# GpSimd, not VectorE, adds row and mask of the mLSTM decays; a split wait and two reordered steps in a hybrid streaming layer

## The reference

```python
dm = where(tril, bh[:, None] - bh[None, :] + ig[None, :], -inf)    # decays
m_t = maximum(bh + m, max(dm, -1))                                 # running maximum
sc = (q @ k.T) * exp(dm - m_t[:, None])
num = sc @ v + exp(bh + m - m_t)[:, None] * (q @ C.T)
h = num / maximum(abs(den), exp(-m_t))[:, None]
```

## Time and profile before

| | |
|---|---|
| median of 3 runs | 944.44 us (944.26 to 945.87) |
| the profiled execution | 944.33 us, its span 942.5 us |
| mean granted clock of TensorE in it | 0.996 |
| TensorE busy | 926.9 us, 98% |
| VectorE / ScalarE / GpSimd busy | 52% / 22% / 47% |
| DMA | 113.02 MB, mean 120 GB/s |

### The profile page before, as it was taken

How to read it: one execution, slowest core, us unless ns; L and a number is a source line. 1 busy time by engine, 2 the same in 40 slices (tenths; PEclk the granted TensorE clock), 3 DMA queues, 4 the chain that set the end, 5 groups by cost and what they waited for, 6 DMA issues and landing times.

```text
span 942.5 us, 14894 instructions
## 1 busy us (share of the span) xinstructions
PE 926.9 (98%) x5718; PEld 813.5 (86%) x5718; DVE 493.8 (52%) x1009; ACT 203.9 (22%) x445; POOL 444.6 (47%) x469
## 2 busy tenths in 40 slices
PE   8999999999999999999999989999999999999998
PEld 6776777777999999999977667777789999999998
DVE  5473645854565656512253555478356565653221
ACT  2223245432100000100031243453320000001001
POOL 6210281033976666676411205603168666666770
PEclk9999999999999999999999999999999999999999
DMA  9958311319544444343443772212474444544321
GB/s 282 253 101 82 123 47 47 91 11 240 146 138 136 135 134 134 125 156 124 121 130 109 55 144 58 77 52 51 79 190 135 135 135 138 144 134 139 130 91 45
DMA packets 159635, 113.02 MB, mean 120 GB/s; under 512 B 10246, under 2 KB 157356, under 8 KB 159436
## 3 DMA queue, kind: packets, MB, share of 16 engines
q1 hardware_dynamic: 154660, 104.50, 38.3%
q0 software_dynamic: 4272, 6.80, 6.9%
q10 hardware_dynamic: 632, 0.75, 0.3%
HBM read 108.46 MB, written 2.27 MB: 117 GB/s over the span
## 4 chain that ended last, share of the span: by engine, by line
PE 89%; DMA 6%; DVE 3%; ACT 1%; issue 1%; POOL 0%; SPq 0%; DVEq 0%; ACTq 0%
PE ps L1126 51%; PE ps L774 14%; PE ps L1083 7%; DMA arena<-r 5%; PE ps L1144 2%; PE ps L883 1%; PE ps L980 1%; PE ps L920 1%; PE ps L822 1%; DMA arena<-in_x_sample 1%; PE ps L1021 1%; PE ps L802 1%; PE ps L1030 1%; PE ps L963 1%; PE ps L1064 0%
## 5 line engine op out<-in xcount | busy, mean ns | idle before, releaser
L774 PE MATMUL ps<-hT,ring 128*128 128x320 f32 x672 | 190.4, 440 | 2.2 <-DVE hT L1595 1.7
L774 PEld LDWEIGHTS ps<-hT,ring 128*128 128x128 f32 x672 | 126.1, 192 | 55.9 <-issue 4.5
L601 POOL TENSOR_TENSOR work<-ring 128x512 f32<-128x512 f32 (+1 forms) x66 | 81.8, 1239 | 153.6 <-issue 113.3
L1126 PE MATMUL ps<-mixT,ring 128*128 128x160 f32 x672 | 105.0, 299 | 0.0
L1126 PE MATMUL ps<-hT,work 128*128 128x160 f32 x672 | 98.5, 299 | 0.0
L1126 PE MATMUL ps<-hT,ring 128*128 128x160 f32 x672 | 98.1, 299 | 0.0
L1126 PEld LDWEIGHTS ps<-mixT,ring 128*128 128x128 f32 x672 | 95.8, 190 | 0.0
L1126 PEld LDWEIGHTS ps<-hT,ring 128*128 128x128 f32 x672 | 93.7, 190 | 0.3
L1126 PEld LDWEIGHTS ps<-hT,work 128*128 128x128 f32 x672 | 93.7, 190 | 0.0
L603 POOL TENSOR_TENSOR work<-ring 128x512 f32<-128x512 f32 (+1 forms) x66 | 82.3, 1248 | 5.2
L602 POOL TENSOR_TENSOR ring<-ring 128x512 f32<-128x512 f32 (+1 forms) x66 | 82.2, 1246 | 5.2
(11 more groups left out here) (392 smaller groups left out, 1351.3 us busy)
## 6 DMA issues: line engine op xcount, KB each, us to landing
ring<-in_w_gu SPq DMA_DIRECT2D x88, 512.0 KB, 5.2
ring<-in_w_in SPq DMA_DIRECT2D x44, 512.0 KB, 6.2
ring<-in_w_down SPq DMA_DIRECT2D x32, 512.0 KB, 4.4
ring<-in_w_out SPq DMA_DIRECT2D x16, 512.0 KB, 4.4
ring<-in_w_down SPq DMA_DIRECT2D x16, 384.0 KB, 3.7
cst<-in_consts POOLq DMA_DIRECT2D x1, 1664.0 KB, 11.6
ring<-in_w_in SPq DMA_DIRECT2D x2, 640.0 KB, 5.6
arena<-r POOLq DMA_DIRECT2D x8, 160.0 KB, 17.1
```

Of the source, the lines that this page charges most:

```text
L601: step(tt(s3, a11, a21, ALU.subtract))
L774: ins = mm(bank(use, 0, T, m), w[:, k, c:c + m], hT[:, k, 0:T], start=(k == 0), stop=(k == KT - 1))
L1126: ins = mm(bank(use, at * HT, HT), left, right(k), start=(opens and k == 0 and at == 0), stop=(closes and k == n - 1), skip_group_check=True)
```

## The change

It has five parts.

1. The broadcasts of heads 0 and 1 count on the semaphore `tables_loaded`, those of heads 2 and 3 on `latents_loaded`. `decay_arg(0)` and `decay_arg(1)` wait for the first two alone, the others for all.
2. `decay_arg` goes from VectorE to GpSimd. There heads 0 and 1 stand behind the signal `b_out`; heads 2 and 3 stand in the loop over states, each ahead of the wait for the state two heads back. Each head but the first waits for the last one's exponentials, since `dmx` is one buffer. ScalarE waits for `w_d` of head h - 2 before it overwrites `dh[h % 2]`.
3. TensorE turns the mLSTM output ahead of `weigh_values(0)` and no longer at the start of head 1.
4. VectorE gates it (`group_out`) ahead of `b_out(0)`, not behind it.
5. ScalarE copies the turned probabilities of head 1 ahead of the second value copy of C.

```diff
@@ setup @@
-        NSMALL = len(SMALL)
+        NTABLES = 16 * (len(SMALL[5::2]) + 1)
@@ GpSimd @@
                 need(pool, "m_rows", l, 1)
+                pool.wait_ge(sem("tables_loaded"), NTABLES + 32 * l)
                 for h in range(H):
-                    pool.dma_start(r2b[h], r2[h:h + 1, :].unsqueeze(1).broadcast_to([1, P, T])).then_inc(sem("latents_loaded"), 16)
+                    arrived = sem("tables_loaded") if h < 2 else sem("latents_loaded")
+                    pool.dma_start(r2b[h], r2[h:h + 1, :].unsqueeze(1).broadcast_to([1, P, T])).then_inc(arrived, 16)
...
+                def decay_arg(h):
+
+                    if h < 2:
+                        pool.wait_ge(sem("tables_loaded"), NTABLES + 32 * (l + 1))
+                    else:
+                        pool.wait_ge(sem("latents_loaded"), 80 * (l + 1))
+                    if h > 0:
+                        need(pool, "decay_d", l, H, h)
+                    for a, q0, n in ((0, 0, 256), (256, 128, 128), (448, 256, 64)):
+                        step(nc.gpsimd.tensor_tensor(dmx[:, a:a + n], r2b[h][:, q0:q0 + n], C("negmask")[:, a:a + n],
+                                                     ALU.add), "dmx" if a == 448 else None)
+
+                decay_arg(0)
+                decay_arg(1)
                 for grp in "dc":
...
                     for h in range(H):
+                        if grp == "d" and h + 2 < H:
+                            decay_arg(h + 2)
                         need(pool, f"state_{grp}", l, H, h + 1)
@@ TensorE @@
-                pe.wait_ge(sem("latents_loaded"), 48 + (48 + 16 * H) * l)
+                pe.wait_ge(sem("latents_loaded"), 48 + 80 * l)
...
                 for h in range(H):
-                    if h == 1:
-                        turn_out("dT", l, ytm, "y_d")
...
+                    if h == 0:
+                        turn_out("dT", l, ytm, "y_d")
                     weigh_values(h)
@@ ScalarE @@
                     need(act, "dmx", l, H, h + 1)
+                    if h >= 2:
+                        need(act, "w_d", l, H, h - 1)
...
                 conv_input(0)
+                probs_copy(1)
                 value_copy("rv", "c", 1)
-                probs_copy(1)
@@ VectorE: decay_arg and its calls go @@
-                def decay_arg(h):
-                    dve.wait_ge(sem("latents_loaded"), (48 + 16 * H) * (l + 1))
-                    ...
-                decay_arg(0)
...
-                    if h + 1 < H:
-                        decay_arg(h + 1)
...
                 maxima(1)
-                b_out(0)
                 need(dve, "gate_d", l, 1)
                 group_out(l, "dT", 6, True)
+                b_out(0)
```

More of the change, by code:

```diff
@@ L684, in _ @@
                         if l == 0:
-                            pool.wait_ge(sem("tables_loaded"), 16 * (len(SMALL[5::2]) + 1))
+                            pool.wait_ge(sem("tables_loaded"), NTABLES)
                         need(pool, "decay_d", l, H)
@@ L924, in _ @@
                     pe.wait_ge(sem("small_loaded"), 16 * len(SMALL[4::2]))
-                    pe.wait_ge(sem("tables_loaded"), 16 * (len(SMALL[5::2]) + 1))
+                    pe.wait_ge(sem("tables_loaded"), NTABLES)
                     pe.wait_ge(sem("consts_loaded"), 16 * 5)
@@ L1804, in _ @@
                     dve.wait_ge(sem("small_loaded"), 16 * len(SMALL[4::2]))
-                    dve.wait_ge(sem("tables_loaded"), 16 * (len(SMALL[5::2]) + 1))
+                    dve.wait_ge(sem("tables_loaded"), NTABLES)
                 need(dve, "glb", l, 1)
@@ L1816, in tails @@
                     return v.tensor_tensor(vw[:, h % 2, :, 0:e], vaug[:, :, h, 0:e], end, ALU.mult)
-                def decay_arg(h):
-                    dve.wait_ge(sem("latents_loaded"), (48 + 16 * H) * (l + 1))
-                    for a, q0, n in ((0, 0, 256), (256, 128, 128), (448, 256, 64)):
-                        step(v.tensor_tensor(dmx[:, a:a + n], r2b[h][:, q0:q0 + n], C("negmask")[:, a:a + n], ALU.add),
-                             "dmx" if a == 448 else None)
                 def d_out(h):
```

## The result

The changed kernel takes 948.24 us (median of 5 runs, 947.71 to 949.06) against 944.45 for the kernel before (5 runs, 944.26 to 946.17): a ratio of 1.0035, with a 95% interval of 1.0022 to 1.0048. It is slower, by 3.8 us. The forecast was 945.7, no measurable change, in a range up to 947.6.

A forecast was written before the change was run, and what follows sets the result against it. TensorE, busy 98% of the span, bounds the kernel. Later head 0 weights 2 x 1.5, less 1.2 for reorders and 0.4 for clock, give +1.4 us: 945.7 us, from a profiled 944.33, range 943.6 to 947.6.

The forecast's parts named there:

- (g): Clock behind TensorE's stand: less work falls in the low stretch, 0.4 us given back; bounds 0.8 back, 3.4 lost.
- (a): Split wait: GpSimd, held by its output landings, starts head 0's addition at 92.0, 0.6 us later; the split buys nothing.
- (b): Addition on GpSimd: 1.67 us for three pieces, 1.72 with ScalarE's wake-up, against VectorE's 1.05; 0.67 more on the chain.
- (c): Head 0's tails on VectorE beside GpSimd's next addition: 0.2 us more on the chain, bounds 0 and 0.36.
- (d): Other heads: TensorE isn't held at head 3, whose late addition has 2.6 us of cover.
- (e, f): Earlier mLSTM output turn and ScalarE copy: short waits at L786 and L1037 go, 1.2 us back, bounds 0 and 1.6.
- R3: Rival: the small edits (reorders) don't help, 1.2 us not given back, 946.9 us; chance 0.08.
- R2: Rival: longer stand costs one more low clock stretch, 1.7 us; 947.4 in one layer, 949.1 in both; chance 0.12.
- R1: Rival: the split works, head 0's addition begins before about 87, TensorE's wait goes, 10.1 less, 934.3 us; chance 0.07.
- R4: Rival: head 3's addition comes late behind state outputs landing after 111.6; 947.7 us if 1 us late; chance 0.03.
- R5: Rival: the chain to head 0's weights isn't longer, 944.2 us, no change; included in the main forecast's 0.70.

The follow-up runs named there:

- E6: Changed kernel without the split, every addition on GpSimd waiting for all four broadcasts: 948.54 us, ratio 1.0028 to the kernel before.
- E3: Changed kernel with the two small outputs (`p_mm`, `s_mm`) issued behind the additions of heads 0 and 1: 934.04 us, ratio 0.9883 to before.
- E2: Kernel before with the reordered steps alone: 940.82 us, ratio 0.9956.
- E4: Changed kernel with 16 extra identity matmuls in front of TensorE's wait at head 0 in each layer: 943.01 us, ratio 0.9969 to before.
- E9: Kernel before with 11 extra identity matmuls in front of TensorE's wait at head 0 in each layer: 940.92 us, ratio 0.9959.
- E5: Changed kernel without the reordered steps, so split wait and addition on GpSimd alone: 949.50 us, ratio 1.0041 to before.
- E7: Changed kernel with the two small outputs behind the additions and no split: 946.82 us, ratio 1.0003 to before.
- E8: Kernel before with the split wait and all reordered steps, addition left on VectorE: 933.50 us, ratio 0.9871.
- E10: Changed kernel with 16 extra identity matmuls before TensorE's wait at head 0 in layer 1 only: 946.25 us, ratio 1.0006 to before.
- E11: Repeat of the changed kernel with the two small outputs behind GpSimd's additions, on one chip with the VectorE version: 933.90 us.

## Why the prediction was wrong

The step that failed is (g), the clock: I took 0.4 us given back, and the profile shows 1.7 lost, 2.1 of the 2.5 us by which the forecast of 945.7 missed. The rest of the miss is 0.4 outside the span and 0.5 between the profiled run and the median, less 0.5 that the reorders gave back beyond my figure.

- *(a) GpSimd's start.* Right, and shown. 91.93 against 92.0 predicted; the profile names `out_s_mm`, E6 shows that the split has no effect there, E3 that moving the two outputs releases it. In layer 1 the start was later still, 553.75: 1.15 after VectorE's 552.60 there; 0.33 of that is the layer's own delay, so 0.8.
- *(b) The addition on GpSimd.* Right: 1.66 us for the three pieces against 1.67 by the earlier trace rows.
- *(c) Two engines at one time.* Half right. The tails took 0.36 in layer 0, as before, and 0.46 in layer 1: 0 and 0.1 more where I took 0.2. Another 0.14 came from a place that I hadn't priced: VectorE began the products 0.22 after ScalarE's last piece (95.17), against 0.08 before. GpSimd's next addition began only at 95.46, so this isn't contention; its cause stays open. VectorE's timeline in layer 1:

```profile
557.95 0.46 DVE L1836 TENSOR_TENSOR work<-work 128x195 f32<-128x195 f32 x1
...
560.27 2.51 DVE L1873 TENSOR_TENSOR arena<-arena 128x1792 f32<-128x1792 f32 x1
```

  Together the stand grew by 1.3 and 1.7 us, 3.0 in the sum as forecast.
- *(d) The other heads.* Right: no wait there, and the fourth addition (109.61) was in time. Its margin was thinner than I wrote: the tails of head 3 ended at 113.98, 2.1 us before TensorE came, and not 2.6.
- *(e, f) The reorders.* Right, somewhat larger: 1.0 and 0.7 us by the start of the same instructions in the changed kernel, 1.9 in E2, against 1.2. The 0.16 us at the third weighing of layer 1 is new. R3 is refuted by E2.
- *(g) The clock.* This step failed. I took 0.4 given back, the low stretch keeping its place while less work fell in it. In layer 0 the stretch moved with the restart and nothing was given back; in layer 1 a second stretch followed, 1.7 us more (the delay of 3.69 at 568.54 is 1.66 above the 2.03 at 558.55). That is R2 in one layer, to which I gave 0.12, with the mechanism I had named for it. With it the sum for the span closes: 3.0 stood more, 1.7 given back by the reorders, 1.7 clock, 3.0 of span. E4 shows it from the other side: with its clock held up the changed kernel is 0.3% faster than before, and 0.1% slower than before with fillers of its own (E9). My bound for this term went to 3.4 lost, but the range that I gave (up to 947.6) holds R2 in one layer (947.4) by a hair and in both (949.1) not at all: it was narrower than my own bounds.
- *The rest.* 0.4 us of the 3.4 between the profiled runs lie outside the span: 2.1 to 2.3 us of each run lie there in every kernel that has both the additions on GpSimd and the reorders, 1.9 in E5, and 1.8 to 1.9 in the others. No run explains it. The median, 948.24, is 0.5 above the profiled run. The other four runs have mean granted clocks of 0.992 to 0.994 against its 0.994. That some had the double stretch in both layers, or the one near the start that is described below, would fit; no profile shows either.
- *The frame.* I set the forecast against 944.44, the median of three runs of before. In the batches, 51 more runs of it spread from 944.2 to 947.8, many near 944.3 or 946.0, with medians of 945.9 to 946.6; what sets the two levels apart no profile of before shows. Against those the changed kernel is 0.2 to 0.3% slower (E6, the same kernel in effect: 1.0028), nearer to the forecast of 0.13 but above it too.

R1 was the right mechanism in the wrong kernel: its 934.3 us is what E3 (934.04) gives once the outputs are out of the way. E7 shows that both are needed: with the outputs out of the way but no split it is 946.82. R4 and R5 did not come.

The version that beats both kernels is E8: split wait, reordered steps, addition left on VectorE, 933.5 us.

## What to carry to other kernels

Before work moves to another engine, read what that engine is already waiting for at that place, above all a wait for the landing of everything it has sent: here a small output issued behind four large transfers on the same queue landed 23.49 us later, behind all of them. A finer wait is worth only what the engine that holds it can use. And where the busiest engine stands before a long run of matmuls, price the clock as a cost that can double (1.7 us became 3.4 here), not as one that shrinks; a few extra matmuls in the stand are a cheap way to find out how much of a stall is clock.

## What the runs showed of the hardware that I had not expected

- The clock answers to TensorE's standing in steps. 2.75 us of standing gave one low stretch of 3.4 us, in each layer of the profiles of before and E2; 3.6 to 4.5 us gave one or two (nine stands in the profiles of the changed kernel, E5, E6, E7 and E10, five of them two), each worth 1.7 us. Fillers that kept TensorE at work in the stand removed them (E4, E9).
- Another such stretch comes and goes near the start, behind 1.7 us of waiting for the first normalised tiles. In E3's profiled run, 1.5 us above its median, it is there:

```profile
17.20:20.60 3.40, 3.40 (x8) 2.13 (x7) 2.40 (x5) 0.00 (x0) 3.40 (x6) 0.50 1.05 326
```

  The profiles of E4 and E11 have it too; the others have not, though all show the same 1.7 us of waiting.
- When GpSimd's addition and a VectorE instruction with two SBUF inputs met, the one that had begun second paid. These are meetings in the profile of the changed kernel. The first line is VectorE's in layer 0, the second GpSimd's in layer 1:

```profile
98.64 2.02 DVE L1873 TENSOR_TENSOR arena<-arena 128x1792 f32<-128x1792 f32 x1
...
569.70 1.65 POOL L693 TENSOR_TENSOR work<-arena,cst 128x256 f32<-128x256 f32 x3 [1.30 <-DMA out_s_mn<-sst]
```

  In layer 0 VectorE's L1873 began at 98.64 and took 2.02 us, as before; GpSimd's addition began at 98.81 and took 3.39 against 1.66 alone. In layer 1 GpSimd began at 560.17, L1873 at 560.27: L1873 took 2.51, and the addition still 3.32, since its second piece came while L1873 ran. At 569.70 GpSimd began and took its usual 1.65; the tails, begun at 569.78, took 0.86 instead of 0.36. On the chain, where the tails met the addition's second piece at 557.95, they lost 0.1. The Trainium skill (GPSIMD Engine Reference, Key points) states that GpSimd shares its SBUF interfaces with VectorE, with contention beside VectorE instructions that have two SBUF inputs; the rows agree. What no row of before had told is which of the two pays.
